# Modulation weights in two halves, and the first context tile's shift added as products

## The reference, cut to what matters

```python
m = jax.nn.silu(cond) @ w_mod + b_mod            # 1024 -> 6 * 1024; cond is c (latent) or c_ctx (context)
sh1, sc1, g1, sh2, sc2, g2 = jnp.split(m, 6, axis=-1)
h = rmsnorm(x, g_attn) * (1.0 + sc1) + sh1       # "modulate", x is ctx or the latent x
z = h @ w_in                                     # 1024 -> 1184 columns
```

## Time and profile before

| | us |
|---|---|
| median of three runs | 1366.16 (1365.88 to 1367.72) |
| the profiled execution, its own time | 1368.26 |
| its span in the trace | 1366.3 |
| PE busy | 1322.1 (97%) |
| DVE busy | 1022.2 (75%) |
| ACT busy | 737.3 (54%) |
| POOL busy | 510.9 (37%) |
| PE clock, mean share of full speed | 0.991 |

### The profile page before, as it was taken

The page is one execution under the profiler, slowest core; times in us unless marked ns, Lnnn a source line. Parts: engine busy times, 40 slices in busy tenths (PEclk is TensorE's granted clock), DMA queues, the critical chain, the costliest instruction groups (busy, mean ns, idle before and its releaser), DMA issues.

```text
span 1366.3 us, 19011 instructions
## 1 busy us (share of the span) xinstructions
PE 1322.1 (97%) x7118; PEld 1117.9 (82%) x7118; DVE 1022.2 (75%) x1396; ACT 737.3 (54%) x1405; POOL 510.9 (37%) x350
## 2 busy tenths in 40 slices
PE   4899998999999999999999999999999999999998
PEld 0688887889888988898888888888888888888886
DVE  1888777787788777776687796767687776868678
ACT  2756565788877877984223543444353535344440
POOL 2567664021199995411000031404123232404333
PEclk8999999999999999999999999999999999999999
DMA  9565657633156564401334535527261735437053
GB/s 375 181 179 167 176 162 236 200 91 88 27 214 194 154 206 153 107 16 32 93 108 139 174 103 213 189 94 265 83 236 62 250 121 213 157 125 245 31 185 124
DMA packets 149130, 210.55 MB, mean 154 GB/s; under 512 B 10136, under 2 KB 101144, under 8 KB 146224
## 3 DMA queue, kind: packets, MB, share of 16 engines
q1 hardware_dynamic: 144432, 200.91, 45.4%
q10 hardware_dynamic: 4352, 8.39, 1.7%
q0 software_dynamic: 256, 0.05, 0.0%
HBM read 162.90 MB, written 44.32 MB: 152 GB/s over the span
## 4 chain that ended last, share of the span: by engine, by line
PE 73%; DVE 15%; ACT 7%; DMA 2%; issue 1%; SPq 0%; DVEq 0%; ACTq 0%
PE f_ps L2749 19%; PE f_ps L2712 17%; PE a_ps L1449 7%; PE o_ps L1797 6%; PE a_ps L1465 5%; PE a_ps L1495 5%; PE f_ps L2280 5%; ACT s_pr L1546 3%; DVE s_nmx L1631 2%; PE t_ps L977 2%; DMA t_wm<-in_w_mod 1%; PE t_ps L966 1%; PE f_ps L2765 1%; PE t_ps L992 1%; DVE f_fin L2557 1%
## 5 line engine op out<-in xcount | busy, mean ns | idle before, releaser
L2260 POOL TENSOR_TENSOR f_wr<-f_wr,f_wr 128x1024 f32<-128x1024 f32 x24 | 61.8, 2576 | 286.1 <-DMA f_wr<-in_w_mlp 157.3
L2749 PE MATMUL f_ps<-f_bh,f_ah 128*128 128x512 f32 x392 | 152.6, 389 | 0.6 <-DVE mix L2583 0.6
L2749 PE MATMUL f_ps<-f_bh,f_al 128*128 128x512 f32 x392 | 152.5, 389 | 0.0
L2749 PE MATMUL f_ps<-f_bl,f_ah 128*128 128x512 f32 x392 | 152.5, 389 | 0.0
L1645 DVE TENSOR_TENSOR l_pT<-a_ps,l_pT 128x512 fp32r<-128x512 f32 (+1 forms) x192 | 109.0, 594 | 53.2 <-ACT l_pT L1556 53.1
L2581 DVE TENSOR_TENSOR mix<-mix,f_ps 128x512 f32<-128x512 f32 x180 | 116.5, 682 | 37.5 <-PE f_ps L2749 37.2
L1449 PE MATMUL a_ps<-l_k,l_q 96*128 96x512 f32 (+1 forms) x576 | 136.4, 366 | 0.5 <-DVE l_mo L1657 0.5
L977 PE MATMUL t_ps<-w_in,t_h 128*128 128x416 f32 (+2 forms) x600 | 123.8, 352 | 0.0
L1556 ACT ACTIVATE l_pT<-a_ps 128x512 fp32r<-128x512 f32 (+1 forms) x192 | 95.0, 525 | 39.6 <-PE a_ps L1465 39.2
L1563 ACT ACTIVATE l_pr<-a_ps,l_nb 128x256 f32<-128x256 f32 (+1 forms) x128 | 100.5, 790 | 12.5 <-DVE l_nb L1636 10.2
L1449 PEld LDWEIGHTS a_ps<-l_k,l_q 96*128 96x128 f32 x576 | 95.3, 189 | 12.5 <-DVE l_mo L1657 0.7
(11 more groups left out here) (252 smaller groups left out, 2951.2 us busy)
## 6 DMA issues: line engine op xcount, KB each, us to landing
f_hq<-scratch_hs SPq DMA_DIRECT2D x64, 512.0 KB, 5.4
l_wg<-in_w_mod SPq DMA_DIRECT2D x8, 2048.0 KB, 8.4
f_w<-in_w_mlp SPq DMA_DIRECT2D x16, 1024.0 KB, 7.5
f_ring<-scratch_hs SPq DMA_DIRECT2D x32, 512.0 KB, 5.2
f_wr<-in_w_mlp SPq DMA_DIRECT2D x24, 512.0 KB, 3.8
t_wm<-in_w_mod SPq DMA_DIRECT2D x8, 1024.0 KB, 13.0
scratch_k<-t_kT SPq DMA_DIRECT2D x20, 384.0 KB, 3.7
l_k<-scratch_k SPq DMA_DIRECT2D x8, 960.0 KB, 10.3
```

Of the source, the lines that this page charges most:

```text
L2749: last = nc.tensor.matmul(ps[:, b, :], op_a[s][x][:, f, t * P:(t + 1) * P], op_b[s][w][:, f, :], start=(i in (M1, M2, M5) and f == 0 and k ...
```

## The change

The eight loads of modulation weights become eight loads of two row blocks by 1024 columns (1 MB each again): four with the scale columns, then tile 0, a0, a1, tile 1 and the norms, then four with the shift columns, then kv, r0 and the rest. `w_uq` is now issued behind a wait for the last modulation product (its room holds the last two blocks of shift weights).

PE forms the scale half of the modulation (8 steps of two groups), spreads the scale rows, fills tile 0, which now has no shift, makes `project_first`, then the shift half of the modulation (8 steps of two groups), then the products with the low weights. Only then come `turn_shift` (the context's shift row turned into 8 columns), the four shift rows of `spread_row`, and `shift_first`: 24 products that add the context's shift times `w_in` into tile 0's z. DVE finishes `mo` in two halves of 64 partitions; ahead of the shift half it now has the low parts of kv and of r0, which has left the first turn of the loop.

The diff, cut to its core:

```diff
+    shift_col = [small(f"t_shift_col{i}", [P, KC], F32R) for i in range(2)]
+    (turned_shift, TURNED0), (shift_hi, HI0), (shift_lo, LO0) = (silu_ready, 1), (exped, 1), (gains_scaled, 1)
-    spread_bank = (5, 6, 7, 3, 4, 5, 6, 7)
+    spread_bank = (5, 7, 6, 3, 5, 7, 6, 3)
+    def shift_view():
+        return ps[:, UB, 0:4 * 64].rearrange("p (c j r) -> p j c r", c=4, j=2)[:, :, :, 1]
...
@@ sync
-        for k in range(KC - 2):
-            load_wm(k)
+        for n in range(4):
+            load_pair(n, slice(D, 2 * D), wm_scale[:, 2 * n:2 * n + 2, :])
         load_x(0)
-        load_wm(KC - 2)
-        load_wm(KC - 1)
         load_raw("a0")
+        load_raw("a1")
         load_x(1)
-        load_raw("a1")
         sp.dma_start(cols[:, :], A["norm_cols"]).then_inc(gains, 16)
         sp.dma_start(norms[:, :], A["norm_rows"]).then_inc(gains, 16)
+        for n in range(4):
+            load_pair(4 + n, slice(0, D), wm_near[:, 2 * n:2 * n + 2, :] if n < 3 else wm_far[:, :, :])
         load_raw("kv")
         load_raw("r0")
...
         load_raw("r3")
+        sp.wait_ge(wm_used, 2 * KC)
         load_raw("uq")
...
@@ gpsimd, add_shift
             if t == 1:
-                pool.wait_ge(spread_copied, 4)
+                pool.wait_ge(spread_copied, 6)
...
@@ scalar
         high_weights("a0")
-        square_x(1, stx[:, 1:2])
-        high_weights("a1")
         hi_fill("x0", 0)
         hi_fill("x1", 0)
+        high_weights("a1")
+        copy_spread(0)
+        copy_spread(1)
+        copy_spread(2)
+        copy_spread(3)
+        square_x(1, stx[:, 1:2])
         root_x(1)
-        for n in range(4):
-            copy_spread(n)
         high_weights("kv")
         high_weights("r0")
+        act.wait_ge(turned_shift, TURNED0 + 1)
+        nc.scalar.activation(shift_col[0][:, :].rearrange("p (j c) -> p j c", j=2), shift_view(), ACT.Copy).then_inc(shift_hi, 1)
+        for n in range(4, 8):
+            copy_spread(n)
...
@@ scalar, loop over i
-            if i == 0:
-                for n in range(4, 8):
-                    copy_spread(n)
...
@@ vector, modulate_first
+                V.scalar_tensor_tensor(out=x, in0=x, scalar=stx[:, 0:1], in1=ps[:, spread_bank[f], :],
+                                       op0=ALU.mult, op1=ALU.mult).then_inc(h0_ready, 1)
-                link(V.scalar_tensor_tensor(out=x, in0=x, scalar=stx[:, 0:1], in1=ps[:, spread_bank[2 * f], :],
-                                            op0=ALU.mult, op1=ALU.mult))
-                V.tensor_tensor(x, x, ps[:, spread_bank[2 * f + 1], :], ALU.add).then_inc(h0_ready, 1)
@@ vector
+        dve.wait_ge(wm_used, KC)
+        link(V.tensor_tensor(mo[64:P, :], ps[64:P, UB, :], bm[64:P, :], ALU.add))
+        V.tensor_tensor(mo[64:P, :], mo[64:P, :], gm[64:P, :], ALU.mult).then_inc(mod_ready, 1)
         inverse_x(0)
-        dve.wait_ge(wm_used, KC)
-        link(V.tensor_tensor(mo[:, :], ps[:, UB, :], bm, ALU.add))
-        V.tensor_tensor(mo[:, :], mo[:, :], gm, ALU.mult).then_inc(mod_ready, 1)
         modulate_first()
         lo_fill("x0", 0)
         lo_fill("x1", 0)
+        low_weights("a1")
         inverse_x(1)
-        low_weights("a1")
         scale_x(1)
...
         low_weights("kv")
+        low_weights("r0")
+        dve.wait_ge(wm_used, 2 * KC)
+        V.tensor_tensor(mo[0:64, :], ps[0:64, UB, :], bm[0:64, :], ALU.add).then_inc(mod_ready, 1)
+        dve.wait_ge(shift_hi, HI0 + 1)
+        V.tensor_tensor(shift_col[1][:, :].rearrange("p (j c) -> p j c", j=2), shift_view(),
+                        shift_col[0][:, :].rearrange("p (j c) -> p j c", j=2).bitcast(F32), ALU.subtract).then_inc(shift_lo, 1)
...
@@ vector, loop over i
-            if i == 0:
-                low_weights("r0")
...
@@ tensor
+        def modulation(k, js, w):
+            for j in js:
+                last = MM(ps[32 * j:32 * j + 32, UB, :], silu[:, k, :], w[:, j % 2 * BANK:(j % 2 + 1) * BANK],
+                          start=(k == 0), stop=(k == KC - 1))
+            last.then_inc(wm_used, 1)
         def spread_row(n):
-            r, j = 1 - n // 4, (2, 0, 3, 1)[n % 4]
+            r, j = 1 - n // 2 % 2, (2 if n < 4 else 0) + n % 2
+            rows = slice(64 * (j // 2), 64 * (j // 2) + 64)
-            MM(ps[:, spread_bank[n], :], ident[:, 32 * j + r:32 * j + r + 1].to_broadcast([P, P]), mo[:, :],
+            MM(ps[:, spread_bank[n], :], ident[rows, 32 * j + r:32 * j + r + 1].to_broadcast([64, P]), mo[rows, :],
                start=True, stop=True).then_inc(spread, 1)
+        def turn_shift():
+            for c in range(4):
+                last = nc.tensor.transpose(ps[:, UB, 64 * c:64 * c + 64], mo[0:64, c * P:(c + 1) * P], ident[0:64, 0:64])
+            last.then_inc(turned_shift, 1)
+        def shift_first():
+            pe.wait_ge(shift_lo, LO0 + 1)
+            for k in range(KC):
+                for i, (a, x) in enumerate(((0, 0), (0, 1), (1, 0))):
+                    ins = MM(ps[:, ZB, 0:NA], shift_col[a][:, k:k + 1].to_broadcast([P, P]), w_in[x][:, k, 0:NA],
+                             start=False, stop=(k == KC - 1 and i == 2))
+            ins.then_inc(z_ready, 1)
...
+        for k in range(KC):
+            pe.wait_ge(wm_loaded[k // 2], 16)
+            modulation(k, (2, 3), wm_scale[:, k, :])
+        pe.wait_ge(mod_ready, 1)
+        spread_row(0)
+        spread_row(1)
+        fill("x0", 0)
+        fill("x1", 0)
+        spread_row(2)
+        spread_row(3)
+        project_first()
+        for k in range(KC):
+            pe.wait_ge(wm_loaded[4 + k // 2], 16)
+            modulation(k, (0, 1), wm_shift(k))
+        project_first_low()
+        pe.wait_ge(mod_ready, 2)
+        turn_shift()
+        for n in range(4, 8):
+            spread_row(n)
+        shift_first()
...
@@ tensor, loop over i
-            if i == 0:
-                for n in range(4, 8):
-                    spread_row(n)
```

More of the change, by code:

```diff
@@ L146, in token_phase @@
     zs = room("t_z", [P, IN_W])
-    wm_in = {i: Z.room(at, skip)(f"t_wm{i}", [P, n, 2 * D]) for i, at, skip, n in ((0, "H", 0, 4), (4, "L", 0, 3), (7, "T", 9984, 1))}
-    wm = [wm_in[i][:, k - i, :] for k in range(KC) for i in (0, 4, 7) if 0 <= k - i < (4, 0, 0, 0, 3, 0, 0, 1)[i]]
+    wm_scale = Z.room("H")("t_wm_scale", [P, KC, D])
+    wm_near = Z.room("L")("t_wm_near", [P, KC - 2, D])
+    wm_far = Z.room("T")("t_wm_far", [P, 2, D])
+    wm_shift = lambda k: wm_near[:, k, :] if k < KC - 2 else wm_far[:, k - KC + 2, :]
     room = Z.room("L", 6144)
@@ L723, in modulate_first @@
                 x = xr[:, 0, f * BANK:f * BANK + BANK]
[L724 to L728 removed]
+                dve.wait_ge(spread, f + 1)
+                V.scalar_tensor_tensor(out=x, in0=x, scalar=stx[:, 0:1], in1=ps[:, spread_bank[f], :],
+                                       op0=ALU.mult, op1=ALU.mult).then_inc(h0_ready, 1)
         def low_weights(j):
@@ L1007, in up_kv @@
                 ins.then_inc(u_ready, 1)
[L1009 to L1013, removed]
+        def modulation(k, js, w):
+            for j in js:
+                last = MM(ps[32 * j:32 * j + 32, UB, :], silu[:, k, :], w[:, j % 2 * BANK:(j % 2 + 1) * BANK],
                           start=(k == 0), stop=(k == KC - 1))
             last.then_inc(wm_used, 1)
-        pe.wait_ge(ident_loaded, 16)
-        pe.wait_ge(mod_ready, 1)
         def spread_row(n):
-            r, j = 1 - n // 4, (2, 0, 3, 1)[n % 4]
-            if n >= 5:
-                pe.wait_ge(spread_copied, n - 4)
-            MM(ps[:, spread_bank[n], :], ident[:, 32 * j + r:32 * j + r + 1].to_broadcast([P, P]), mo[:, :],
+            r, j = 1 - n // 2 % 2, (2 if n < 4 else 0) + n % 2
+            if n >= 4:
+                pe.wait_ge(spread_copied, n - 3)
+            rows = slice(64 * (j // 2), 64 * (j // 2) + 64)
+            MM(ps[:, spread_bank[n], :], ident[rows, 32 * j + r:32 * j + r + 1].to_broadcast([64, P]), mo[rows, :],
                start=True, stop=True).then_inc(spread, 1)
-        for n in range(4):
-            spread_row(n)
-        fill("x0", 0)
-        fill("x1", 0)
         def project_first():
@@ L1042, in project_first @@
                     pe.wait_ge(w_lo, 1)
-                ins = MM(ps[:, ZB, 0:NA], hT[0][:, k, :], w_in[1][:, k, 0:NA], start=False, stop=(k == KC - 1))
-            ins.then_inc(z_ready, 1)
-        project_first()
+                MM(ps[:, ZB, 0:NA], hT[0][:, k, :], w_in[1][:, k, 0:NA], start=False, stop=False)
+        def turn_shift():
[8 more added lines that the diff above has]
+                             start=False, stop=(k == KC - 1 and i == 2))
+            ins.then_inc(z_ready, 1)
+        pe.wait_ge(silu_ready, 1)
+        for k in range(KC):
+            pe.wait_ge(wm_loaded[k // 2], 16)
+            modulation(k, (2, 3), wm_scale[:, k, :])
+        pe.wait_ge(ident_loaded, 16)
+        pe.wait_ge(mod_ready, 1)
[5 more added lines that the diff above has]
+        spread_row(3)
+        project_first()
+        for k in range(KC):
```

(5 more changed lines are left out.)

17 lines of the change are left out of this document (7 added, 10 removed).

## The result

The change makes the kernel slower: median 1375.89 us of ten runs (1370.54 to 1378.13) against 1366.24 of ten before (1365.20 to 1368.43), ratio 1.0059, 95% interval 1.0048 to 1.0071. That is 9.65 us between the medians and about 8 by the ratio; the forecast was 5.0 and its range ended at 1373.4. The runs also lie much further apart than before: three at 1370.5 to 1371.1, five at 1377.3 to 1378.1, two between. The profiled execution is one of the upper five: 1377.33, span 1375.3, 9.07 over the profiled one of before.

A forecast was written before the change was run, and what follows sets the result against it. PE, busy 1322.1 of 1366.3 us, was taken as the bound, so a late start stays. `project(1, 0)` 2.9 us late plus 2.1 for the clock made 5.0 on 1366.16: 1371.2 us, range 1367.6 to 1373.4.

The forecast's parts named there:

- the added products: `shift_first` on PE, 24 products of 416 columns ahead of z: 4.82 us, bounds 4.8 to 6.
- little given back later: After the start, r0's low part leaving DVE's first turn gives back 0 us, bound 0.9.
- PE's clock: PE idle 36.1 to 39.9 drops to the low clock, slowing the work behind: 2.1 us, up to 3.1.
- r0's landing: r0's load lands at 35.6 us, as before, with the same loads ahead; the forecast rests on it.
- the shorter rows: Weight loads with rows of 4 KB instead of 8 KB: 0 to 0.7 us later, taken as 0.
- the four spreads: The four late `spread_row` products on PE, now ahead of z: 3.43 us.
- The price of one product over 64 rows: Late spreads on PE read 64 rows, not 128: full price taken, bound half that (1.7 us less).
- one event with one chance (0.62): Main case: delay of 2.2 to 3.6 us plus clock loss of 1.4 to 3.1, giving 1369.8 to 1372.9 us.
- the steps said to end nowhere: Scale half through `project_first`, ending near 27.5 us, 14 us before its old place; none of it reaches the end.
- the clock holds: Rival, chance 0.14: no clock fall behind PE's pause, only the 2.9 us delay remains, 1369.1 us.
- Worse: Rival, chance 0.07: 4 KB rows and repeated column at their bounds (0.7 + 1.2), second low period: 1374 us.
- the start might not gate on r0: Rival, chance 0.17: r0 lands early, bias add at 34.8, `project(1, 0)` at 49.1, 0.9 us earlier: 1365.3 us.

The follow-up runs named there:

- the kernel with both pauses filled: The change plus unused products in two PE waits: two before the scale rows, twenty before the shift is turned; median 1372.40 us.
- The reordered version: The change with bias add before kv's and r0's low parts, two late spreads behind z, then two unused early products and 128-row late spreads: 1367.30 us, ratio 1.0001.
- first kernel: The change with both parts of r0's split put back behind the shift; median 1370.90 us, ratio 1.0024 to the kernel before.
- second: The change with r0's split put back behind the shift and two unused products in PE's wait for the scale rows; 1369.66 us, ratio 1.0021.

## Why the prediction was wrong, point by point

The direction, the place and the chain were right: r0 in front of the bias add, PE idle from 36.4 to 40.7 (36.1 to 39.9 forecast), the spreads and the added products on the path, 4.30 us from z to the next tile's product (4.3 forecast), little given back later. **The step that failed is the last term of the sum, *PE's clock*, taken at 2.1 us; the profiled run paid 5.7.** Term by term, z came at 55.10 and not at the 48.6 that the sum had without the clock:

- r0's landing and the steps behind it: 0.8 late. I had bounded the shorter rows at "0 to 0.7 us later, and I take 0"; the landing was 1.1 late, of which the kernel before with rows of 4 KB shows 0.8. The low part took 1.76 instead of 1.9.
- `turn_shift`: 0.48, forecast 0.45.
- the four spreads: 7.07 instead of 3.43, all at the low clock.
- the added products: 6.87 instead of 4.82, two thirds of that time at the low clock. At the high clock they took 4.81 to 4.83 in five other kernels, as `project(1, 0)` does (5.09 and 5.12 in two where spreads over 128 rows stand ahead, which they overlap), so the repeated column costs nothing and its bound of 6 was not needed.

0.8 + 3.6 + 2.05 = 6.5, the whole difference. The last two, 5.7 us, are the clock's price in the profiled run; between medians it was 5.3. I had taken 2.1 and allowed 1.4 to 3.1. Of the 4.4 us by which the start came later than forecast (59.40 against 52.9 + 2.1), 3.6 are this term and 0.8 the landing. The reasoning was that the pause brings a low period of 3.4 us, since the three falls shown in the earlier trace rows were of about that length, and that PE's steady work behind the pause would end it. What I left out is the fourth low period of that same trace. The rows shown have 0.73 from 30 to 40 us, and the stretch before it was lower still:

```profile
20.00:30.00 10.00, 4.93 (x24) 0.56 (x24) 1.67 (x4) 3.99 (x5) 0.00 (x0) 0.59 1.02 409
```

(1 - 0.59) / 0.5 x 10 + (1 - 0.73) / 0.5 x 10 = 8.2 + 5.4 = 13.6 us, through the last modulation products (32 output rows per group), the pauses between them and most of the first spreads. I took the short length from places where products over 128 rows followed and put it on spreads over 64. With 128 rows behind the pause it came to 3.4 us in one kernel and to 6.9 in another: the estimate fits the first, is half of the second and a quarter of this one.

The price of one product over 64 rows was right: 3.65 us for four against 3.70 over 128. The rule in the Trainium skill, "TensorE: Matmul & The Clock Gate" (section "Why this matters for your kernels"), that fewer rows make a single product no faster, holds here. The product itself costs the same; what it costs through the clock was not in the sum.

The second miss is the spread between runs. I treated the fall as one event with one chance (0.62), behind the pause at 36 us. There are two places, and the first, at 17 us, was among the steps said to end nowhere. If the clock falls there, everything up to the shift's products comes 4 to 6 us later (three profiles) and covers all or most of the wait behind r0; the second fall, the costly one, came in none of the three. The change's profiled execution took the second; the profiles of the experiments showed both.

Of the rivals, *the clock holds* (1369.1) might seem to be what the fastest runs of the change show (1370.5 to 1371.1). Their mean clock speaks against it: 0.993, close to the 0.991 or 0.992 of the upper five, where the kernel with both pauses filled has 0.996 in four of its five runs. They are more likely runs with the early fall, which went away when the first pause was filled; none was profiled. The case without a fall is that kernel, at 1372.40, 5.6 us over the kernel before and not 2.9; its profile has r0's high part start at 37.88, 2.3 later than forecast. *Worse* (1374) had a second low period, not one long one. That the start might not gate on r0 is refuted by the landing, the chain and the two kernels with r0 put back.

**What stays open.** With r0 put back, medians stay 3 us above the kernel before although the start in their profiles is equal to it. Their runs with a mean clock of 0.996 or more have medians only 0.5 us (first kernel) and 2.0 us (second) above it, so a part of the 3 us is low clock. The reordered version is 2 us ahead at the start and equal in the median. The kernel before was itself profiled in one of its slower runs (1368.26 against 1366.2), so profiles and medians compare different runs: the profiled times with r0 put back, 1368.33 and 1368.48, are equal to that one. What its faster runs do better was not seen: its mean clock was 0.991 in the profiled run, 0.990 to 0.992 in its runs near 1366.5 and 0.992 in those under 1366, so the clock tells them apart by little. No run here settles it, and so it is not shown what the added products and the halved steps cost in the median. Whether one unused product in the first pause would do was not tried.

## What to carry to other kernels

Before moving a wait ahead of matrix work, ask what stands behind the pause: the pause costs time of its own (2.7 us between medians here), and the clock's fall doubles the time of everything PE does until it rises (5.3 us here). In these profiles the low period was two to four times as long behind spreads over 64 rows as behind products over 128. Take the length of a low period from the place in the trace whose products have the shape of those that will follow, and count every pause of a microsecond or two in the start as a place where a run may fall. When runs of one kernel lie in two groups, compare their mean clocks, and fill a suspected pause with unused products: the group that goes away belongs to that pause.

## What the runs showed of the hardware that was not expected

- A full row of 128 partitions or half of it: the same 3.7 us for four spreads at the high clock, but 7.06 us (41.23 to 48.29) with 64 rows and 4.58 (41.61 to 46.19) with 128 behind the same pause of 4 us, since the clock stayed at 1.2 GHz for 13.7 and 3.4 us. With the added products over 128 rows directly behind such a pause it was 6.9 us.

```profile
41.23 7.14 PE L1032 MATMUL t_ps<-t_mo,ident 64*128 64x512 f32 x8
48.29 7.12 PE L1062 MATMUL t_ps<-w_in,t_shift_col 128*128 128x416 f32 x24
```

```profile
41.61 5.14 PE L1032 MATMUL t_ps<-t_mo,ident 128*128 128x512 f32 x8
46.19 5.12 PE L1062 MATMUL t_ps<-w_in,t_shift_col 128*128 128x416 f32 x24
```

- The clock fell near 20 us behind a pause of 1.7 us, followed by spreads over 64 rows, in three profiles out of six with that pause; in the profiles of the five kernels with that pause filled there was none. In the kernel before it fell at about 21.8 us with pauses of 1.41 and 1.44 us between short modulation products before it.
- Loads of the same bytes ran at 407 GB/s with rows of 4 KB and at 423 with rows of 8 KB.
